# Two transformer blocks on one NeuronCore: the silu of each convolved slab one place earlier in ScalarE's program, and the delta rule started 30 ticks into the projection instead of 25

## The reference

```python
p = h @ w_in
qkv = jax.nn.silu(causal_depthwise_conv(p[..., Q_OFF:Z_OFF], conv_qkv_w))     # 4 taps, 1536 columns
q, k, v, z = ...                                                             # 4 heads of 128
g = -exp(a_log) * softplus(a + dt_bias);  beta = sigmoid(b)
o = gated_delta_rule_chunked(l2_normalize(q), l2_normalize(k), v, g, beta)    # chunks of 64 tokens
o = rms_norm(o, gdn_norm_w) * jax.nn.silu(z)
y_sc = sc_b * causal_depthwise_conv(sc_c * sc_h, conv_short_w)                # 3 taps
return jnp.concatenate([y_gdn, y_sc], axis=-1) @ w_out
```

## Time and profile before

| | |
|---|---|
| runs | 2089.39 us median of 3 |
| the profiled execution's own time | 2089.39 us |
| its span in the profile | 2088.2 us |
| mean granted TensorE clock | 0.97 |
| PE busy | 1940.8 us, 93% |
| POOL busy | 954.8 us, 46% |
| ACT busy | 710.3 us, 34% |
| DVE busy | 686.0 us, 33% |
| HBM | 87 GB/s over the span |

### The profile page before, as it was taken

One profiled execution on the slowest core, in us unless ns is written; L12 is line 12 of the kernel. 1 busy time (PEld: TensorE's weight loads), 2 busy tenths in 40 slices (PEclk: granted clock), 3 DMA queues, 4 the chain that ended last, 5 costly groups with the idle time before them and its releaser, 6 DMA issues.

```text
span 2088.2 us, 32887 instructions
## 1 busy us (share of the span) xinstructions
PE 1940.8 (93%) x13928; PEld 1655.1 (79%) x13928; DVE 686.0 (33%) x1069; ACT 710.3 (34%) x1093; POOL 954.8 (46%) x1257
## 2 busy tenths in 40 slices
PE   5989998999999999999999899977777799999997
PEld 4667776777888889999999899966666478888885
DVE  5654454223111102332210156544554422222101
ACT  2563222332222323222222334354445432322222
POOL 3543232545545665554545465421112265555563
PEclk9999999999999999999999999988989899999998
DMA  7332231233333232223222322000000323323221
GB/s 281 123 135 87 67 104 65 81 111 121 121 91 96 91 96 91 91 92 91 89 88 88 126 91 87 31 7 2 2 2 2 131 81 103 99 91 96 90 100 58
DMA packets 54690, 182.75 MB, mean 88 GB/s; under 512 B 6512, under 2 KB 6768, under 8 KB 54416
## 3 DMA queue, kind: packets, MB, share of 16 engines
q1 hardware_dynamic: 54544, 180.65, 26.6%
HBM read 175.39 MB, written 5.24 MB: 87 GB/s over the span
## 4 chain that ended last, share of the span: by engine, by line
PE 83%; DVE 6%; ACT 4%; DMA 3%; issue 2%; POOL 1%; SPq 1%; DVEq 0%; ACTq 0%
PE PS L498 69%; PE PS L615 3%; PE PS L969 1%; DMA RAWS<-w_w_in 1%; DMA ADA<-w_ada 1%; PE PS L962 1%; POOL WL L2171 1%; PE PS L976 1%; DMA BON<-bsave 1%; PE PS L987 1%; PE PS L533 1%; DMA RAWS<-w_f0g 1%; PE PS L634 0%; DVE HL L1585 0%; PE PS L943 0%
## 5 line engine op out<-in xcount | busy, mean ns | idle before, releaser
L2171 POOL TENSOR_TENSOR WL<-RAWS,WH 128x256 fp32r<-128x256 f32 x1074 | 824.2, 798 | 780.2 <-ACT WH L1666 780.1
L498 PE MATMUL PS<-HH,WH 128*128 128x264 f32 (+2 forms) x2184 | 668.8, 348 | 42.6 <-POOL WL L2171 9.4
L498 PE MATMUL PS<-HL,WH 128*128 128x264 f32 (+2 forms) x2184 | 655.3, 342 | 0.0
L498 PE MATMUL PS<-HH,WL 128*128 128x264 f32 (+2 forms) x2184 | 653.1, 341 | 0.0
L498 PEld LDWEIGHTS PS<-HH,WH 128*128 128x128 f32 (+1 forms) x2184 | 377.7, 190 | 108.6 <-issue 22.7
L1666 ACT ACTIVATE WH<-RAWS 128x1024 fp32r<-128x1024 f32 (+2 forms) x275 | 283.7, 1033 | 475.2 <-PE PS L498 401.1
L498 PEld LDWEIGHTS PS<-HH,WL 128*128 128x128 f32 (+1 forms) x2184 | 378.4, 190 | 48.4 <-issue 0.6
L498 PEld LDWEIGHTS PS<-HL,WH 128*128 128x128 f32 (+1 forms) x2184 | 378.9, 190 | 47.7 <-issue 2.1
L498 PE MATMUL PS<-IHf,WH 128*128 128x512 f32 (+1 forms) x704 | 209.4, 338 | 0.0
L498 PE MATMUL PS<-IHf,WL 128*128 128x512 f32 (+1 forms) x704 | 209.3, 338 | 0.0
L498 PE MATMUL PS<-ILf,WH 128*128 128x512 f32 (+1 forms) x704 | 209.2, 338 | 0.0
(11 more groups left out here) (498 smaller groups left out, 1814.7 us busy)
## 6 DMA issues: line engine op xcount, KB each, us to landing
RAWS<-w_w_in SPq DMA_DIRECT2D x52, 512.0 KB, 4.4
RAWS<-w_ada SPq DMA_DIRECT2D x32, 512.0 KB, 3.6
RAWS<-w_f0g SPq DMA_DIRECT2D x22, 512.0 KB, 3.6
RAWS<-w_f0u SPq DMA_DIRECT2D x22, 512.0 KB, 3.7
RAWS<-w_f1g SPq DMA_DIRECT2D x22, 512.0 KB, 3.6
RAWS<-w_f1u SPq DMA_DIRECT2D x22, 512.0 KB, 3.5
RAWS<-w_f2g SPq DMA_DIRECT2D x22, 512.0 KB, 3.5
RAWS<-w_f2u SPq DMA_DIRECT2D x22, 512.0 KB, 3.6
```

Of the source, the lines that this page charges most:

```text
L498: ins = te.matmul(ps[0:m, q, o:o + b - a] if len(halves) > 1 else ps[0:m, o:o + b - a], w[:, k * m:k * m + m], v[:, k0 + k, a:b], start=fi ...
L2171: ins = ge.tensor_tensor(WL[s % NS][:, p], RAW[i % NR][:, p], WH[s % NS][:, p].bitcast(f32), ALU.subtract)
```

## The change

Four edits. `DELTA_TICKS` is 30 instead of 25. In the loop over slabs 1 to 9 ACT applies `silu(i - 1)` right behind `evict(i - 1)`, where it was `silu(i - 2)`. `silu(9)` stands behind `l2_roots(4)` ahead of the woven part; `silu(10)` and `silu(11)` stand at the start of slabs 11 and 12, right after the split of the next slab, before the eight ticks. And `log_and_exp()`, the explicit table load, stands once ahead of the woven part instead of behind `silu(11)`.

```diff
-DELTA_TICKS = 25
+DELTA_TICKS = 30
...
-            if i > 1:
-                silu(i - 2)
+            silu(i - 1)
...
         begin("w_in", IN_ORDER[10], 1)
         evict(9)
-        silu(8)
         begin("w_in", IN_ORDER[11], 1)
         l2_roots(4)
+        silu(9)
...
                 begin("w_in", j, 1 if i < 24 else 2)
+                if 10 < i < 13:
+                    silu(i - 1)
                 for _ in range(8):
                     yield
                 if i < 12:
                     evict(i)
-                    silu(i - 1)
                     continue
...
-                    if i == 12:
-                        silu(11)
-                        log_and_exp()
...
         pr, dr = project_rest(), later_by(DELTA_TICKS, pipeline(4, prepare, scan))
+        log_and_exp()
         alternate(pr, pr, dr, dr, pr, pr, dr, dr, dr)
```

## The result

The changed kernel takes 2105.02 us (2103.61 to 2108.41, four executions), the kernel before 2087.99 in the same session: 1.0079 times as long, 95% interval 1.0061 to 1.0096. The prediction was 2098.5 with a range up to 2104. The direction and the mechanism of the first part were right; the size was not: 9.1 us were forecast and 17 came.

A forecast was written before the change was run, and what follows sets the result against it. Bound by a slackless load-split-eviction-convolution loop in the first slabs, then by PE's work in the woven part. 8.4 + 1.8 - 1.1 = 9.1 us on 2089.39 gave 2098.5 us; 8-in-10 range 2091 to 2104.

The forecast's parts named there:

- Part 1, the loop: First slabs: ScalarE waits for each convolution, steps of 6.6 to 6.7 us; slab 12 split 5.8 to 6.2 us later.
- Part 2, the second roots: Silu 9 and two table loads precede slab 10's eviction, 3.2 us; delta rule starts 11.3 later, 8.4 of it lag.
- Part 3, the woven part: Projection and delta rule woven, shifted four projection ticks: PE is full, two waits go and two come, +1.8 us.
- -1.4, -1.2, +2.4 and +2.0: Woven part's waits: first short-convolution block's bank gone, `VBT` gone, third block ahead of L1234, last block ahead of last `VN`.
- other orders: Woven part: possible new collisions between orders in the four engines' programs, allowed at 2 us each way.
- Part 4, the end: Wait for `HL` before `w_out`: -4.0 us for the block gone, +2.9 for moved matmuls, sum -1.1 us.
- The clock: Longer waits before slabs 9 and 13 may bring PE's 1.2 GHz level: 0 to 1.3 us, 0 in the sum.
- A: Front hidden because the convolution wait only replaces the load wait: 2085.7 us, or +0.7 with both new waits; chance 0.10.
- B: Half absorbed: loop keeps 5.8 us, second roots and slab 13 add none, woven part +0.9; 2094 us, chance 0.18.
- D: Each table switch stalls ScalarE 1.4 us beyond its load, 2.8 more for two loads: 2101 us, chance 0.04.
- C: More waits and lower clock: 9.1 plus 1.3, 1.3, 1.0 (L1349) and 1 of collisions, 13.7 us; 2103 us, chance 0.13.
- The forecast's own mark for being wrong: Slab 9's split near 108, delta rule before 158, or new waits between 162 and 350 summing over 6 us.

The follow-up runs named there:

- second profile of before: The kernel before, unedited, profiled once more; this execution took 2080.74 us, where the first profiled one took 2089.39.
- the quick execution: First profiled execution of the kernel before with only DELTA_TICKS changed from 25 to 30: 2092.49 us, against that kernel's median of 2100.98.
- the ticks alone: The kernel before with DELTA_TICKS 30 instead of 25 and nothing else: 2100.98 us, ratio 1.0064.
- 28 ticks: The kernel before with DELTA_TICKS 28 instead of 25 and nothing else: 2084.38 us, ratio 0.9998.

## Why the prediction was wrong

*Part 1, the loop: right as a mechanism on ScalarE.* Steps of 6.6 us, waits of 3.3 us for the convolution, slab 9's split 5.1 later where 5.8 was told. The edit alone cost 7 us where 4.5 to 6 were expected, but not all of that is this lag. In its profile slab 12 is split 4.6 us later, counted from slab 0, but L680 starts only 3.4 us later than in the second profile of before (1.1 than in the first), since PE makes up part of the lag. The other 3.5 us up to `w_out` come behind L680, with 0.7 us more of waits and 10 us lost to the clock instead of 7.

*Part 2, the second roots: near in the sum, wrong in one piece.* L680 starts 11.8 us later, 11.3 forecast; against the second profile of before it is 14.2, so that the two numbers are this close is partly luck. Slab 13's split came earlier than worked out, PE was done with slab 12 earlier still, the wait for slab 13 was 4.05 and not 2, and its six matmuls ran at half rate.

*Part 3, the woven part: the step that failed.* Its terms were -1.4, -1.2, +2.4 and +2.0, sum +1.8. The first three came as -1.4, -0.9 and +2.9. Missing is `iv0LD`, 3.2 us in two waits, of 0.88 and 2.31. VectorE's timeline in the changed kernel ahead of the longer one:

```profile
271.65 0.68 DVE L1313 TENSOR_TENSOR VBT<-PS,COLT 128x512 f32<-128x512 f32 x1
272.25 1.51 DVE L1056 SCALAR_TENSOR_TENSOR ACC<-RAWS,CA,ACC 128x1024 f32<-128x1024 f32 x1
273.68 1.23 DVE L1341 SCALAR_TENSOR_TENSOR QKV<-QKV,CV,RSTD 128x512 f32<-128x512 f32 x1
274.94 0.69 DVE L1344 TENSOR_TENSOR QKV<-QKV,Z 128x512 f32<-128x512 f32 x1
275.55 0.42 DVE L1230 TENSOR_TENSOR iv0UD<-UU,KC 128x256 f32<-128x256 f32 x1
275.88 0.68 DVE L1217 TENSOR_TENSOR YS<-YS,PS 128x512 f32<-128x512 f32 x1
276.48 0.42 DVE L1234 TENSOR_TENSOR iv0LD<-PS,KC 128x256 f32<-128x256 f32 x1
```

VectorE is busy without a gap for 5 us. Before, the modulation slab (L1056) and L1217 stood behind L1237 of this inverse:

```profile
266.93 0.42 DVE L1234 TENSOR_TENSOR iv0LD<-PS,KC 128x256 f32<-128x256 f32 x1
...
267.59 0.41 DVE L1237 TENSOR_TENSOR iv0XU<-iv0UD,KC 128x256 f32<-128x256 f32 x1
267.93 1.75 DVE L1056 SCALAR_TENSOR_TENSOR ACC<-RAWS,CA,ACC 128x1024 f32<-128x1024 f32 x1
269.85 0.69 DVE L1217 TENSOR_TENSOR YS<-YS,PS 128x512 f32<-128x512 f32 x1 [0.17 <-PE PS L498]
```

The shift put both ahead, 1.5 + 0.6 us, and L1341 takes 1.23 us instead of 0.74. The shorter wait, at 183.55, is of the same kind: a modulation slab of 1.28 us (181.54) stands ahead of L1234 of the first inverse, where before it stood ahead of the first L1310. I had followed the four short-convolution blocks and neither L1056 nor L1217, which are moved past the same places. The allowance of 2 us for "other orders" was too small for these 3.2. The waits of this part sum to 3.2 + 2.9 - 1.4 - 0.9 = 3.8, and 3.9 is what the table of positions shows from L680 to the last block, against the second profile of before. Against the first, which has the same waits and lost less to the clock, it is 6.5, so that they agree to 0.1 is luck.

The +2.0 before the last `VN` was right as a mechanism (2.87 instead of 0.78 in the quick execution), but in the other the last block costs 8.9 us by the lower clock in its place.

*Part 4, the end.* Forecast -4.0 for the block that is gone and +2.9 for the moved matmuls. From the last L756's start (349.34 before, 373.01 after) to `w_out` it is 9.4 us before and 6.3 after, a gain of 3.1 for the 4.0: PE also came there earlier, and waited 1.6 us instead of 2.8.

*The clock.* "0 to 1.3 us; the sum takes 0" was the other step that failed: the last block alone lost 8.9 us to it in the changed kernel's profile. I looked for it behind the two long waits of the front and argued from a mean of 0.98 that the woven part does not lose it. But 0.98 over 185 us is already 4 us, in two stretches of 10, so the woven part did lose it. With more waits it lost more in most profiles, though not in all.

*The rivals.* A and B fell at L680. D fell with the table loads. C came nearest: it named the 1.2 GHz level and more waits. It was 2 us too low: its clock was two stretches of 1.3 us, its 1.0 for L1349 is 0.2 in the profile of the ticks alone, and its 1.0 of collisions was 3.2. The forecast's own mark for being wrong, new waits between 162 and 350 us of more than 6 us, was met, though barely and with one of the two forecast: 3.2 and 2.9.

*Open.* Where the clock falls in one execution. The same kernel has executions with and without the loss (2091 and 2104), and the profile of 28 ticks has a low stretch in the last block too (0.60 from 340 to 355) without being slower than before in the median. That filling the waits brings the clock back is shown, and that the median grows with the sum of the waits in these kernels; which wait sets off which stretch is not, and neither is how much of the 17 us is clock.

## What to carry to other kernels

When a shift moves one stream against another by some ticks, list every operation of the moved stream on each engine and look at what each now stands in front of, the cheap ones and those of a third purpose too; the next number (28 for 30) may be free where this one costs 15 us. Where PE does many small matmuls with waits of one to three us between them, price a us of new wait at more than itself (2.5 us by the medians here, 1.2 to 3.0 in single executions), since part of the cost is a lower clock. And take a second profile before explaining 10 us: a kernel's profiled execution may be its quickest.

## What the runs showed of the hardware

In the kernel with 30 ticks, where PE waits for other engines, 8 us of added matmuls that nobody uses made the median 6 us lower (2101.0 to 2095.0) at a mean clock of 0.973 instead of 0.967; in the kernel before the same matmuls changed it by no more than the noise. The 1.2 GHz level comes in stretches of 5 to 20 us at places that differ between executions of the same program: in the kernel before at 220 to 230 and 245 to 255 in one profile, and at 305 to 330 in the other. A filler of 128 by 128 with 128 columns in fp32r took 0.115 us at full clock.
